# Sample rows of both mixers laid as four groups of two sequences; HGRN2's state products in four row groups

## The reference

```python
S_t = diag(exp(log_f_t)) @ S_{t-1} + k_t v_t^T ;  o_t = S_t^T q_t
# per chunk, b = cumsum(log_f):
o     = att @ v + (q * exp(b)) @ S              # att: scores with pairwise decays, causal
S_new = exp(b_last) * S + (k * exp(b_last - b))^T @ v
```

## Time and profile before

| | |
|---|---|
| median of 3 runs | 3076.22 us (3073.29 to 3076.69) |
| the profiled execution | 3078.22 us, its span 3076.4 us |
| granted clock of the core | 0.992 |
| PE / PEld busy | 98% / 92% |
| DVE / ACT / POOL busy | 56% / 42% / 10% |
| chain that ended last, by engine | PE 41%, DVE 1%, DMA, ACT and issue 0% |
| DMA | 685.60 MB, 223 GB/s on the mean |

### The profile page before, as it was taken

How to read it: one execution, slowest core, us unless ns; L and a number is a source line. 1 busy time by engine, 2 the same in 40 slices (tenths; PEclk the granted TensorE clock), 3 DMA queues, 4 the chain that set the end, 5 groups by cost and what they waited for, 6 DMA issues and landing times. The chain is left out here.

```text
span 3076.4 us, 65619 instructions
## 1 busy us (share of the span) xinstructions
PE 3014.1 (98%) x26670; PEld 2831.1 (92%) x26670; DVE 1734.4 (56%) x2478; ACT 1305.1 (42%) x1712; POOL 299.0 (10%) x291
## 2 busy tenths in 40 slices
PE   7899999999999999999999999999999999999999
PEld 3689999989899999999999899998999999999998
DVE  2577766765744444444445767766664454454545
ACT  1455555553533343333333544544354343343433
POOL 0112111111300000000001402210130000000001
PEclk8899999999999999999999999999999999999999
DMA  9888888888786686776875875675575555555552
GB/s 376 278 267 261 257 269 272 273 291 267 261 284 209 212 261 213 236 239 205 259 247 172 271 236 183 195 239 181 172 245 165 165 167 167 165 166 165 165 165 93
DMA packets 541653, 685.60 MB, mean 223 GB/s; under 512 B 22236, under 2 KB 469268, under 8 KB 541084
## 3 DMA queue, kind: packets, MB, share of 16 engines
q1 hardware_dynamic: 485650, 627.66, 63.5%
q10 hardware_dynamic: 55732, 54.01, 5.4%
HBM read 650.91 MB, written 30.67 MB: 222 GB/s over the span
## 5 line engine op out<-in xcount | busy, mean ns | idle before, releaser
L1998 DVE TENSOR_TENSOR w_lo<-raw,w_hi 128x1024 fp32r<-128x1024 f32 x804 | 991.4, 1236 | 1147.0 <-ACT w_hi L1366 1143.8
L1366 ACT ACTIVATE w_hi<-raw 128x1024 fp32r<-128x1024 f32 x804 | 849.7, 1059 | 1490.3 <-PE main L615 1183.5
L613 PE MATMUL main<-a_hi,w_hi 128*128 128x288 f32 x4224 | 1273.6, 302 | 8.1 <-DVE a_lo L2554 7.2
L615 PE MATMUL main<-a_hi,w_lo 128*128 128x288 f32 x4224 | 1248.6, 296 | 0.0
L614 PE MATMUL main<-a_lo,w_hi 128*128 128x288 f32 x4224 | 1248.3, 296 | 0.0
L613 PEld LDWEIGHTS main<-a_hi,w_hi 128*128 128x128 f32 x4224 | 795.7, 188 | 43.2 <-issue 26.8
L614 PEld LDWEIGHTS main<-a_lo,w_hi 128*128 128x128 f32 x4224 | 796.1, 188 | 4.5 <-issue 1.9
L615 PEld LDWEIGHTS main<-a_hi,w_lo 128*128 128x128 f32 x4224 | 796.0, 188 | 0.0
L615 PE MATMUL main<-act_hi,w_lo 128*128 128x288 f32 x2048 | 604.9, 295 | 0.0
L614 PE MATMUL main<-act_lo,w_hi 128*128 128x288 f32 x2048 | 604.6, 295 | 0.0
L613 PE MATMUL main<-act_hi,w_hi 128*128 128x288 f32 x2048 | 603.6, 295 | 0.0
(11 more groups left out here) (351 smaller groups left out, 2013.9 us busy)
## 6 DMA issues: line engine op xcount, KB each, us to landing
raw<-in_w_ada SPq DMA_DIRECT2D x384, 512.0 KB, 4.9
raw<-in_w_up SPq DMA_DIRECT2D x256, 512.0 KB, 4.6
raw<-in_w_down SPq DMA_DIRECT2D x256, 512.0 KB, 3.6
raw<-in_hg_w_in SPq DMA_DIRECT2D x128, 512.0 KB, 6.6
raw<-in_gla_w_in SPq DMA_DIRECT2D x100, 512.0 KB, 4.4
raw<-in_hg_w_out SPq DMA_DIRECT2D x32, 512.0 KB, 8.1
gl_s<-in_state_gla ACTq DMA_DIRECT2D x32, 512.0 KB, 5.4
out_new_gla_sample<-gl_s ACTq DMA_DIRECT2D x32, 512.0 KB, 4.4
```

The costliest lines, as they stand in the source:

```text
L613: mm(out, hi, x_hi[:, kb, :], start=kb == 0, stop=False)
L615: last = mm(out, lo, x_hi[:, kb, :], start=False, stop=kb == KB - 1)
L1366: F(w_hi[:, st.split_slot(g)].rearrange("p k n -> p (k n)"), raw[:, slot, :], ACT.Copy).then_inc(hi_ready, 1)
L1998: V.tensor_tensor(w_lo[:, s].rearrange("p k n -> p (k n)"), raw[:, slot, :], w_hi[:, s].rearrange("p k n -> p (k n)").bitcast(F32), ALU.su ...
```

## The change

The 32 sample rows are laid as four groups of 32 partitions (128 in all): a group has the 8 tokens of two sequences, four times over, one for each term of the split product. DVE writes these rows before the transposition: eight small operations at the end of hg_key_mul (one small multiplication less there), and for GLA gl_value_rows at step 17 and four operations in gl_key_mul. The threefold copies on ACT and DVE and the subtractions behind the transposition go. PE waits for the rows (s_split) before hg_sample_turn and before GLA's like transpositions. Two masks by parity (pmask) replace the eight by sequence, hg_vsm is 128 x (2 x 128) a head, and gl_mask is done twice a head.

HG's state products become, for each head of the pair, four matmuls of 32 rows and 256 columns in four row groups and four banks, at steps 9 and 10; DVE reads two halves (eight operations) at each. In the last pair they stand before products 7 and 8, and the wait for ss_read stands before product 11. The samples' scores are four 8 x 8 blocks a head in place of two 32 x 32, and DVE takes four pieces of a level in place of two. In GLA a sample product is two matmuls of 32 rows in two row groups and two banks; read-outs 0 and 1 are both at step 23, 2 and 3 both at step 5, each pair behind all four loads; loads and stores are split by key half, 16 and 16 transfers of 256 KB a head, the next head's loads at steps 6 to 9. The core of the diff:

```diff
+    pmask = mem.put("pmask", [P, 2])
...
+    def term_rows(rows, c):
+
+        return rows.rearrange("p a (g c i) -> p a g c i", g=4, c=4)[:, :, :, c, :]
+
+    def token_groups(v):
+
+        return v.rearrange("p a (g i) -> p a g i", i=8)
...
-                    sample_scores(64 * L + 32 * h, lhs[:, h, TP:T], rhs[:, h, TP:T])
+                    for g in range(4):
+                        own, at = slice(TP + 8 * g, TP + 8 * g + 8), 64 * L + 32 * h + 8 * g
+                        mm(b6[32 * g:32 * g + 8, at:at + 8], lhs[:, h, own], rhs[:, h, own],
+                           start=True, stop=True, skip_group_check=True, tile_position=(0, 32 * g))
...
         def hg_sample_turn(pn):
...
+            pe.wait_ge(H["s_split"], pn + 1)
             for j in range(4):
-                last = turn_samples(b7, j * P, hg_s3[:, j])
+                last = turn(b7[:, j * P:(j + 1) * P], hg_s3[:, j], ident[:, :])
...
-        def hg_last_state(x):
-
-            pn, (h, half_) = HG_PAIRS - 1, divmod(x, 2)
+        def hg_states(pn, h):
+
             pe.wait_ge(H["s_masked"], 2 * pn + h + 1)
-            if x == 0:
+            for g, bank in enumerate((b4, b6, b5, b7)):
+                r = slice(32 * g, 32 * g + 32)
+                last = mm(bank[:, 0:256], hg["tk"][r, h, :], hg["vsm"][r, h].rearrange("p b v -> p (b v)"), start=True, stop=True,
+                          tile_position=(32 * g, 0))
+            last.then_inc(H["ss_done"], 1)
+
+        def hg_last_state(h):
+
+            pn = HG_PAIRS - 1
+            if h == 0:
                 pe.wait_ge(H["ps_read"], pn + 1)
-            elif x == 1:
+                pe.wait_ge(H["rstd_ready"], 2 * pn + 2)
                 pe.wait_ge(ada_copied, ADA_HGO)
-            elif x == 2:
                 pe.wait_ge(mod_ready, ADA_HGO)
             else:
-                pe.wait_ge(H["ss_read"], 4 * pn + 1)
-            mm((b4, b5, b7, b4)[x][:, :], hg["ts"][:, 2 + h, :],
-               hg["vsm"][:, h, 4 * half_:4 * half_ + 4, :].rearrange("p b v -> p (b v)"), start=True, stop=True
-               ).then_inc(H["ss_done"], 1)
-
-        def hg_sample_state(pn, x, ada_count):
-
-            h, half_ = divmod(x, 2)
-            pe.wait_ge(H["s_masked"], 2 * pn + h + 1)
-            if x == 0:
+                pe.wait_ge(H["ss_read"], 4 * pn + 2)
+            hg_states(pn, h)
+
+        def hg_sample_state(pn, h, ada_count):
+
+            if h == 0:
                 pe.wait_ge(H["ps_read"], pn + 1)
-            elif x == 1:
+                pe.wait_ge(H["rstd_ready"], 2 * pn + 2)
+                pe.wait_ge(ada_copied, ada_count)
                 pe.wait_ge(H["o_read"], 2 * pn + 2)
-            elif x == 2:
-                pe.wait_ge(ada_copied, ada_count)
             else:
                 pe.wait_ge(H["ss_read"], 4 * pn + 2)
-            mm((b4, b7, b5, b7)[x][:, :], hg["ts"][:, 2 + h, :],
-               hg["vsm"][:, h, 4 * half_:4 * half_ + 4, :].rearrange("p b v -> p (b v)"), start=True, stop=True
-               ).then_inc(H["ss_done"], 1)
+            hg_states(pn, h)
...
-                if 8 <= s <= 11:
-                    hg_sample_state(pn, s - 8, ADA_HG + n)
+                if s in (9, 10):
+                    hg_sample_state(pn, s - 9, ADA_HG + n)
...
-            for x in range(4):
-                hg_last_state(x)
-                hgo_product(7 + x)
-            for s in range(11, 31):
+            for h in range(2):
+                hg_last_state(h)
+                hgo_product(7 + h)
+            for s in range(9, 31):
+                if s == 11:
...
-            for b in (2 * q, 2 * q + 1):
-                pe.wait_ge(G["s0_loaded"][b % 4], 32 * n + 16 * (b // 4 + 1))
+            if q % 2 == 0:
+                for loaded in G["s0_loaded"]:
+                    pe.wait_ge(loaded, 64 * n + 32 * (q // 2 + 1))
             if q == 0:
                 pe.wait_ge(G["kd_ready"], n + 1)
-                pe.wait_ge(G["s_split"], 2 * n + 2)
+                pe.wait_ge(G["s_turned_read"], 2 * n + 2)
...
-        def gl_sample(n, b):
-
-            pe.wait_ge(G["s_masked"], 8 * n + b + 1)
-            if b == 0:
+        def gl_sample(n, k):
+
+            pair, j = divmod(k, 2)
+            if k == 0:
+                pe.wait_ge(G["s_masked"], 2 * n + 2)
                 pe.wait_ge(G["level_read"], 9 * n + 9)
                 pe.wait_ge(G["turned_read"], 3 * n + 3)
             else:
-                pe.wait_ge(G["ss_read"], 8 * n + b)
-            for j, bank in enumerate((b4, b5)):
-                last = mm(bank[:, :], gl["ksm"][:, b % 2, j, :], gl["vs"][:, :], start=True, stop=True)
+                pe.wait_ge(G["ss_read"], 8 * n + k)
+            for i, bank in enumerate((b4, b5)):
+                g = 2 * (pair // 2) + i
+                r = slice(32 * g, 32 * g + 32)
+                last = mm(bank[:, :], gl["ksm"][r, pair % 2, j, :], gl["vs"][r, :], start=True, stop=True,
+                          tile_position=(32 * g, 0))
             last.then_inc(G["ss_done"], 1)
...
-                if s in (1, 4, 5):
-                    gl_read_out(pn, 1 if s == 1 else s - 2)
+                if s == 5:
+                    gl_read_out(pn, 2)
+                    gl_read_out(pn, 3)
...
-        def gl_load(n, b):
-            act.dma_start(gl["s0"][:, b % 4], gl_state[cols(n, 1), b].rearrange("h k j v -> (h k) j v")
-                          ).then_inc(G["s0_loaded"][b % 4], 16)
-
-        def gl_store(n, b):
-
-            act.wait_ge(G["ss_read"], 8 * n + b + 1)
-            act.dma_start(gl_state_out[cols(n, 1), b].rearrange("h k j v -> (h k) j v"), gl["s1"][:, b % 2]
-                          ).then_inc(G["s_stored"][b % 2], 16)
+        def pair_sequences(pair):
+            return [4 * (pair // 2) + pair % 2 + 2 * i for i in range(2)]
+
+        def gl_load(n, pair, j):
+            for b in pair_sequences(pair):
+                act.dma_start(gl["s0"][:, b % 4, j], gl_state[cols(n, 1), b, :, j, :].rearrange("h k v -> (h k) v")
+                              ).then_inc(G["s0_loaded"][2 * (pair % 2) + j], 16)
+
+        def gl_store(n, k):
+
+            pair, j = divmod(k, 2)
+            act.wait_ge(G["ss_read"], 8 * n + k + 1)
+            for i, b in enumerate(pair_sequences(pair)):
+                act.dma_start(gl_state_out[cols(n, 1), b, :, j, :].rearrange("h k v -> (h k) v"), gl["s1"][:, i, j]
+                              ).then_inc(G["s_stored"][j], 16)
...
-                for q in (0, 32):
-                    mask = masks[q:q + 32, L, :].unsqueeze(1).to_broadcast([32, 2, 32])
-                    V.copy_predicated(hg["atts"][q:q + 32, :, :], mask,
-                                      b6[q:q + 32, 64 * L:64 * L + 64].rearrange("p (h t) -> p h t", h=2))
+                for g in range(4):
+                    r, own = slice(32 * g, 32 * g + 8), slice(8 * g, 8 * g + 8)
+                    mask = masks[r, L, 0:8].unsqueeze(1).to_broadcast([8, 2, 8])
+                    V.copy_predicated(hg["atts"][r, :, own], mask,
+                                      b6[r, 64 * L:64 * L + 64].rearrange("p (h t) -> p h t", h=2)[:, :, own])
...
-            step(V.tensor_tensor(hg_s3[:, 2:4], threefold(hg["x"][:, 1, :, TP:T]), threefold(hg["k"][:, :, TP:T]), ALU.mult))
-            V.tensor_tensor(hg["x"][:, 1], hg["x"][:, 1], hg["k"][:, :, :], ALU.mult)
+            step(V.tensor_tensor(hg["x"][:, 1], hg["x"][:, 1], hg["k"][:, :, :], ALU.mult))
             dve.wait_ge(H["qz_set"], 1)
             for h in range(2):
                 last = V.tensor_tensor(hg["qz"][:, h].rearrange("p b (q c) -> p b q c", c=36)[:, :, :, 0:TB],
                                        hg["qd"][:, h, :].rearrange("p (q b t) -> p b q t", b=2, t=TB),
                                        hg["q"][:, h, TP:T].rearrange("p (q b t) -> p b q t", b=2, t=TB), ALU.mult)
             last.then_inc(H["kd_ready"], 1)
+            dve.wait_ge(panel_read["A"], HG.emptied(n, 2)[1])
+            values, keys = hg_s3[:, 0:2], hg_s3[:, 2:4]
+            v, k = token_groups(hg["v"][:, :, TP:T]), token_groups(hg["x"][:, 1, :, TP:T])
+            V.tensor_copy(term_rows(values, 1).bitcast(F32R), v)
+            V.tensor_copy(term_rows(keys, 1).bitcast(F32R), k)
+            V.tensor_copy(term_rows(values, 3).bitcast(F32R), v)
+            V.tensor_copy(term_rows(keys, 2).bitcast(F32R), k)
+            V.tensor_copy(term_rows(values, 0), v)
+            step(V.memset(term_rows(keys, 0), 0.0))
+            V.tensor_tensor(term_rows(values, 2).bitcast(F32R), v, term_rows(values, 1), ALU.subtract)
+            V.tensor_tensor(term_rows(keys, 3).bitcast(F32R), k, term_rows(keys, 1), ALU.subtract).then_inc(H["s_split"], 1)
...
-            dve.wait_ge(H["s_split"], pn + 1)
+            dve.wait_ge(H["s_turned_read"], pn + 1)
             for h in range(2):
-                V.tensor_tensor(hg["vsm"][:, h],
-                                hg["ts"][:, h, :].bitcast(F32).unsqueeze(1).to_broadcast([96, NB, P]),
```

(78 more changed lines are left out.)

107 lines of the change are left out of this document (55 added, 52 removed).

## The result

The changed kernel takes 3102.31 us (median of 6 runs, 3098.94 to 3107.14); the kernel before, with three more runs beside it, 3075.57. The ratio is 1.0089, 95% interval 1.0079 to 1.0100: slower by 26.7 us. The forecast was 3095, range 3080 to 3106; so +18.8 was forecast and the measured loss is 7.9 larger.

A forecast was written before the change was run, and what follows sets the result against it. PE, busy 98%, was taken as the bound. HG updates 9.8, sample rows 1.8, output projection 3.9, opening 0.8 and GLA 2.5 sum to 18.8 on 3078.22: 3097.0, less 2.0 for the median gives 3095.0 us, range 3080 to 3106.

The forecast's parts named there:

- Bound by PE's sum of work and stalls: Whole kernel: PE is busy 98% of the span, so time is its work plus few stalls; new stalls move all that follows.
- State products on PE: HG pairs: four matmuls side by side make an island of 0.43 us; two a pair are 0.86, 0.10 less than before.
- row price of a switch: Islands on PE: changing tile shape in and out, with its weight load, costs 0.29 us, read from a profiled island.
- DVE's eight updates before step 10: Steady HG pairs: PE waits about 1.1 us at step 10; 1.4 a pair stays in all, seven pairs +9.8.
- The rest that I put at step 11: Steady HG pairs: of the 1.4 us delay a pair, what remains beyond 1.1 at step 10 falls at step 11.
- Sample rows: HG's sample turn: PE waits for eight small DVE operations, 0.25 us a pair, +1.8 over seven pairs.
- Output projection: HG's output projection: PE stalls 2.5 us at product 8's island; with 1.5 for clock, less 0.1, +3.9.
- clock term: HG's output projection: the stall is followed by a stretch of lower clock, 1.5 us within the +3.9.
- Copies in levels: Opening levels: four copy_predicated in place of two, four extra pieces not hidden, +0.8 us; steady pairs have room.
- GLA: GLA stage: PE saves 1.2 us a head, but waits on loads and the tail outweigh it, net +2.5.

The follow-up runs named there:

- half-updates run: The changed kernel with half of HGRN2's state updates on DVE left out, PE's work unchanged: +22.3 us against the kernel before (ratio 1.0065).
- b_shifted: The kernel before with only an unused 32-byte tensor a partition behind bmask, moving all buffers behind it: +6.6 us against the kernel before (ratio 1.0019).

## Why the prediction was right, point by point

- *Bound by PE's sum of work and stalls*: held. What the table above shows before 1724 us is waits, wider islands, the addresses and, in the opening, a stretch of lower clock.
- *State products on PE*: side by side as taken, 0.39 for four. An island costs 0.51, not 0.43, so two a pair are 0.09 more and not 0.10 less than four of 0.23. The row price of a switch carried over roughly. The Trainium skill, TensorEngine Tiling (Array Packing), Theoretical Speedup, gives up to four times the throughput; here the cost of the island ate all of that, as the sum assumed.
- *DVE's eight updates before step 10*: they ended 3.29 us after the split's start, 3.30 forecast, and PE stood for 0.86 (1.1 forecast). The half-updates run gives 0.93 a pair as their price, 1.4 forecast. The rest that I put at step 11 did not come: PE had 0.24 less to do there, because the state product of step 11 is gone, and level 1 was in time.
- *Sample rows*: 0.33 a pair lost (0.25 forecast). Together the pair is 1.35 where the sum had 1.65.
- *Output projection*: wait of 2.1 as placed (2.5). The clock term of 1.5 was taken as certain. It is not: the traced execution shows none, another with the same gap shows it. And the low stretch of before, on which the sum was built up, is absent too, which lowered the traced loss by some 1.5.
- *Copies in levels*: I priced four extra pieces in the opening (+0.8) and said that steady pairs had room. The opening costs 1.2 for them (1.4 with four pieces, 0.2 with two). The room in the steady pairs was there: with the changed kernel's order no wait on them stands in a pair. It is gone once the states come first (0.45 a pair). What was missing is GLA: its levels have the doubled pieces too, PE's waits on level results there grew from 1.7 to 3.6, and the sum had no term for them.
- *GLA*: wrong in its parts. The 1.2 a head that I let PE save is in no trace; the islands of an undisturbed head lose 0.3. My 0.21 for a sample product was also below what the rows give for 512 columns (0.24), and the product costs 0.16 more than before where I had it at nothing or a gain. The net of +2.5 stands against 4.8 here and 4.7 to 8.5 over the traces. I had put the waits on loads; they are 1.4, while those on DVE's results are 7.2 where before has 4.6 on DVE's masks.
- *MLP stages*: no term at all. 3.4 us of the traced loss come from 32 bytes in the memory plan, and b_shifted puts this one line at +6.6 in the median.

So the sign and the main cause, PE waiting for DVE's regrouped updates, were right. That the sum of 18.8 came so near the traces' 20.7 is luck: the pairs (8.8 over all seven, against 11.6) and the projection (0.8 against 3.9) were too high by 6, and GLA, the opening and the addresses together too low by as much.

## What to carry to other kernels

Where one engine has no slack, a regrouping is priced by the latest result it asks for, on the engine that makes it: two groups of eight updates with a wait between them cost more than four of four, though DVE had less to do in all. Small pieces cost their fixed price, so count operations, not elements. After any change of the memory plan compare stages that were not touched. If they moved, the addresses are a suspect, and a run of the old kernel with padding alone tells. Before a part is priced from two traces, compare their granted clocks there.

## What the runs showed of the hardware

- With act_hi and act_lo 32 bytes further on in each partition, the products on them take 133.328 ns from start to start on the mean in place of 132.775, and those on buffers that did not move are unchanged (132.75). By groups it shows on act_hi with w_hi (603.6 to 607.2 us) and hardly on act_lo. Which property of the address matters was not tried.
- DVE's copy_predicated of 8x16 elements takes 0.18 us, of 32x64 0.22.
- Four matmuls of 32 rows and 256 columns, in four row groups and four banks, take 0.39 us together; one such island between full products costs 0.51.
- Behind the same gaps of PE (1.04 and 0.62; 2.1), the granted clock was 1.00 in one execution and 0.50 to 0.54 in another. The same output projection was about 1.4 us shorter in three other traces than in that of before, whose clock fell there. A term for the clock is a chance, not a cost, and single traces differ by it.
